# Two-stack transformer on one core: how TensorE is carried from one sublayer to the next

## What is computed

```python
x = x + rmsnorm(m, g[1])                       # m: attention (layer 0) or short convolution (layer 1)
f = sq_relu_mlp(rmsnorm(x, g[2]), w_mlp_up[i], w_mlp_down[i])
x = x + rmsnorm(f, g[3])
gate = sigmoid(rmsnorm(x, g[4]) @ w_ple_gate[i])
e = (p[i] @ w_ple_proj[i]) * gate
x = x + rmsnorm(e, g[5])
```

## Time and profile before

| | |
|---|---|
| median of 3 runs | 1717.42 us |
| lowest, highest | 1690.49, 1718.61 us |
| span of the profiled execution | 1691.7 us |
| TensorE matmuls busy | 1567.7 us (93%) |
| VectorE, ScalarE, GpSimd busy | 979.4, 724.6, 136.1 us |
| mean granted TensorE clock | 0.938 of full |

### The profile page before, as it was taken

How to read it: one execution, slowest core, us unless ns; L and a number is a source line. 1 busy time by engine, 2 the same in 40 slices (tenths; PEclk the granted TensorE clock), 3 DMA queues, 4 the chain that set the end, 5 groups by cost and what they waited for, 6 DMA issues and landing times.

```text
span 1691.7 us, 24256 instructions
## 1 busy us (share of the span) xinstructions
PE 1567.7 (93%) x9802; PEld 1373.8 (81%) x9802; DVE 979.4 (58%) x1251; ACT 724.6 (43%) x931; POOL 136.1 (8%) x112
## 2 busy tenths in 40 slices
PE   7999999977998999868989999989999799899998
PEld 7966899866988999657668888879999686689997
DVE  4554565555566655549776565655655475456554
ACT  4443554445445544435632222244444363345443
POOL 2000111100000111000212212000000020000000
PEclk8999999988999999988988999989999896699999
DMA  7612465543654555524530000026565352045553
GB/s 252 187 61 76 144 213 186 191 145 123 189 162 156 198 187 187 163 100 124 170 112 26 1 2 1 1 86 208 169 210 174 127 189 64 13 162 189 186 163 124
DMA packets 81823, 229.15 MB, mean 135 GB/s; under 512 B 11729, under 2 KB 17553, under 8 KB 81713
## 3 DMA queue, kind: packets, MB, share of 16 engines
q1 hardware_dynamic: 81584, 227.54, 41.7%
q0 software_dynamic: 128, 0.07, 0.0%
HBM read 226.46 MB, written 1.05 MB: 134 GB/s over the span
## 4 chain that ended last, share of the span: by engine, by line
PE 87%; DVE 8%; ACT 3%; issue 1%; POOL 1%; DMA 1%; SPq 0%; DVEq 0%; ACTq 0%; POOLq 0%
PE PS L404 50%; PE PS L407 33%; PE PS L419 4%; ACT SH L376 1%; DVE X L619 1%; DVE SL L382 1%; DVE LG L1341 1%; DVE XL L518 1%; ACT JK L597 0%; DVE XN L596 0%; DVE XI L1061 0%; POOL SM L609 0%; DVE SL L379 0%; DVE XT L1349 0%; DVE XT L1350 0%
## 5 line engine op out<-in xcount | busy, mean ns | idle before, releaser
L382 DVE SCALAR_TENSOR_TENSOR SL<-ST,SM,SH 128x1024 fp32r<-128x1024 f32 (+1 forms) x256 | 317.0, 1258 | 242.3 <-ACT SH L376 233.9
L404 PE MATMUL PS<-XH,SH 128*128 128x256 f32 x1568 | 443.7, 283 | 8.3 <-DVE XL L518 8.3
L407 PE MATMUL PS<-XH,SL 128*128 128x256 f32 x1568 | 444.5, 283 | 0.0
L404 PE MATMUL PS<-XL,SH 128*128 128x256 f32 x1568 | 443.3, 283 | 0.0
L376 ACT ACTIVATE SH<-ST,SM 128x1024 fp32r<-128x1024 f32 (+1 forms) x256 | 281.1, 1121 | 289.4 <-PE PS L407 271.8
L379 DVE TENSOR_TENSOR SL<-ST,SH 128x1024 fp32r<-128x1024 f32 (+1 forms) x167 | 213.5, 1295 | 171.4 <-ACT SH L376 154.1
L404 PEld LDWEIGHTS PS<-XH,SH 128*128 128x128 f32 x1568 | 301.3, 192 | 10.6 <-ACT XH L517 5.7
L404 PEld LDWEIGHTS PS<-XL,SH 128*128 128x128 f32 x1568 | 298.0, 190 | 0.6
L407 PEld LDWEIGHTS PS<-XH,SL 128*128 128x128 f32 x1568 | 298.1, 190 | 0.0
L376 ACT ACTIVATE SH<-ST 128x1024 fp32r<-128x1024 f32 (+1 forms) x167 | 172.1, 1047 | 193.4 <-PE PS L407 184.4
L404 PE MATMUL PS<-SH,XH 128*128 128x512 f32 (+1 forms) x432 | 178.1, 412 | 29.9 <-ACT XH L517 8.4
(11 more groups left out here) (306 smaller groups left out, 1744.3 us busy)
## 6 DMA issues: line engine op xcount, KB each, us to landing
ST<-in_ffn_w_gu SPq DMA_DIRECT2D x80, 512.0 KB, 4.7
ST<-in_w_mlp_up SPq DMA_DIRECT2D x64, 512.0 KB, 4.7
ST<-in_w_mlp_down SPq DMA_DIRECT2D x64, 512.0 KB, 4.3
ST<-in_ffn_w_down SPq DMA_DIRECT2D x44, 512.0 KB, 4.4
ST<-in_w_attn_in SPq DMA_DIRECT2D x24, 512.0 KB, 3.7
ST<-in_w_conv_in SPq DMA_DIRECT2D x24, 512.0 KB, 3.6
ST<-in_w_ple_gate SPq DMA_DIRECT2D x16, 512.0 KB, 3.6
ST<-in_kv_w SPq DMA_DIRECT2D x16, 512.0 KB, 4.4
```

Source lines behind the costliest of these rows:

```text
L382: b = ve.do(lambda e: e.scalar_tensor_tensor(l[p0:p1, 0:cols], t[p0:p1, 0:cols], sc, h[p0:p1, 0:cols].bitcast(F32), ALU.mult, ALU.subtract ...
L404: pe.go(lambda e: e.matmul(o, l, r, start=start, stop=stop, skip_group_check=skip))
L407: return pe.do(lambda e: e.matmul(o, l, r, start=start, stop=stop, skip_group_check=skip))
```

## The change

- The slots of split weights go from 5 to 6, stages from 5 to 4, parameter rows from 3 to 2, and up to 5 units are split ahead. Head and tail groups of `kind_a` are four units (`EDGE`); a tail has as many as the call gives, and beyond it nothing is split ahead. In a head group the splits are written one by one (`lazy`).
- The functions behind a sublayer are called for one m at a time (`chain(m)`). Two new functions call them: `enter_b` and `enter_a`. Both write, for every engine: chain of m = 0, fill, transposes and split of m = 0, chain of m = 1, and only then, after the first unit has been used on m = 0, the transposes and the split of m = 1.
- `enter_b` (five places) runs its first two units through `kind_b_halves`: each block is multiplied with 128 tokens at a time, so a unit takes 48 matmuls with 128 moving columns where it took 24 with 256.
- `keep_busy` multiplies constants into a free PSUM bank: two or four plain fp32 matmuls of 512 columns in each place, and ten of 128 columns at the start of the kernel.
- In the gates, the embedding's two units stand between the transposes of m = 0 and the chain of m = 1. The sigmoid, its product and the squares are cut into 512-column pieces.
- Lambda and its six DMAs are moved to the beginning of the kernel, behind the forget gate.

```diff
-NSPLIT, NSTAGE, NPAR = 5, 5, 3
+NSPLIT, NSTAGE, NPAR = 6, 4, 2
+EDGE = 4
 LOOK = NSPLIT - 1
...
-    def take_group(n):
+    def take_group(n, look=LOOK):
...
-        while n_split[0] <= min(i + LOOK, len(units) - 1):
+        while n_split[0] <= min(i + max(look, n - 1), len(units) - 1):
             unit_split()
         assert n_split[0] >= i + n
...
-    def kind_a(xs, kbs, banks, first=True, last=True, xt=None, end=False):
+    def kind_a(xs, kbs, banks, first=True, last=True, xt=None, end=False, mid=None, look=LOOK):
...
-        groups = [[k] for k in kbs]
-        if xt is not None and len(kbs) >= 3:
-            groups = [kbs[0:3]] + [[k] for k in kbs[3:]]
-        if end:
-            cut = sum(len(g) for g in groups) - 3
-            groups = [g for g in groups if g[-1] < kbs[0] + cut] + [kbs[cut:]]
+        head = EDGE if xt is not None and len(kbs) >= EDGE else 0
+        tail = min(EDGE, int(end) if end is not True else EDGE)
+        groups = ([kbs[0:head]] if head else []) + [[k] for k in kbs[head:len(kbs) - tail]] + ([kbs[len(kbs) - tail:]] if tail else [])
         assert sum(len(g) for g in groups) == len(kbs)
         for g in groups:
-            us = take_group(len(g))
+            lazy = xt is not None and g is groups[0]
+            us = [] if lazy else take_group(len(g), len(g) - 1 if end and g is groups[-1] else look)
             for m in range(2):
-                if xt is not None and g is groups[0]:
+                if lazy:
                     pe.wait(xt[m])
-                for k, (i, h, l) in zip(g, us):
+                for j, k in enumerate(g):
+                    if lazy and m == 0:
+                        us += take_group(1, 0)
+                    i, h, l = us[j]
                     pe.wait(split_tok[i])
                     for n in range(2):
                         ls = [x[:, k, m * 128:(m + 1) * 128] for x in xs]
                         rs = [x[:, n * 512:(n + 1) * 512] for x in (h, l)]
+                        if first and k == kbs[0]:
+                            pe.wait(bfree[banks[2 * m + n]])
                         tok[m] = mm3(bank(banks[2 * m + n]), ls, rs, first and k == kbs[0], last and k == kbs[-1])
+                    if lazy and mid is not None and m == 0 and j == 0:
+                        mid()
             for i, _, _ in us:
                 pe_done[i] = tok[1]
         return tok
...
+    def kind_b_halves(xs, banks, xt, mid, nblk=8, n=2):
+
+        us = take_group(n, n - 1)
+        for m in range(2):
+            pe.wait(xt[m])
+            for k, (i, h, l) in enumerate(us):
+                pe.wait(split_tok[i])
+                for f in range(nblk):
+                    c = (f % 2) * 256 + m * 128
+                    if m == 0 and k == 0 and f % 2 == 0:
+                        pe.wait(bfree[banks[f // 2]])
+                    ls = [x[:, f * 128:(f + 1) * 128] for x in (h, l)]
+                    rs = [x[:, k, m * 128:m * 128 + 128] for x in xs]
+                    tok = mm3(bank(banks[f // 2], c, c + 128), ls, rs, m == 0 and k == 0 and f % 2 == 0, False)
+                if m == 0 and k == 0:
+                    mid()
+                if m:
+                    pe_done[i] = tok
+
+    def ahead(n=1):
+
+        for _ in range(n):
+            if n_split[0] < len(units) and (n_split[0] < NSPLIT or n_split[0] - NSPLIT in pe_done):
+                unit_split()
+
+    def keep_busy(n, b, c=C_LV, w=512):
+
+        pe.wait(bfree[b])
+        for _ in range(n):
+            mm(bank(b, 0, w), CC[:, 0:128], CC[:, c:c + w], True, True)
+
...
+    keep_busy(10, 7, 0, 128)
...
+    def enter_b(chain, banks, fill):
+
+        r = [None, None]
+        chain(0)
+        keep_busy(*fill[0])
+        r[0] = raw_half(0, 0)
+        chain(1)
+        keep_busy(*fill[1])
+
+        def second():
+            r[1] = raw_half(1, 0)
+
+        kind_b_halves(XS[0], banks, r, second)
+        ahead(1)
+        return raw_rstd()
+
+    def enter_a(chain, base, banks, fill, between=None, **kw):
+
+        r = [None, None]
+        chain(0)
+        keep_busy(*fill)
+        r[0] = raw_half(0, base)
+        if between is not None:
+            between()
+        chain(1)
+        ahead(2)
+
+        def second():
+            r[1] = raw_half(1, base)
+
+        return kind_a(XS[0], range(8), banks, xt=r, mid=second, **kw)
...
+    ve.wait(tl)
+    for j in range(2):
...
+    def mlp(layer, chain, fill, tail_free):
+        rt = enter_b(chain, (4, 5, 6, 7), fill)
...
+            else:
+                t = kind_b(XS[0], range(2, 8), bs, first=False)
...
+        return down(3), pw, (PH, PL), [lb, lc]
...
+        def embed():
+            wait_banks([0, 1, 2, 3])
+            pe.wait(xs_tok)
+            emb.append(kind_a(xs, range(2), (0, 1, 2, 3), look=0))
+
+        tg = enter_a(mlp_chain, 4, (4, 5, 6, 7), (1, 0), embed, end=True)
...
+    rt = enter_b(ple_chain, (4, 5, 6, 7), ((2, 1), (2, 4)))
...
+    kind_b(XS[0], range(2, 4), (4, 5, 6, 7), first=False, last=False)
...
+    before = mlp(1, conv_chain, ((2, 4), (2, 4)), te0[1])
+    ple_chain, _ = ple(1, before)
+    for m in range(2):
+        ple_chain(m)
...
+    def ffn(chain):
+        rt = enter_b(chain, (4, 5, 6, 7), ((1, 2), (2, 3)))
...
+    t = enter_a(chain0, 0, (4, 5, 6, 7), (2, 2))
+    rt = raw_rstd()
```

More of the change, by code:

```diff
@@ L395, in take_group, with take @@
         return [(j, SH[j % NSPLIT], SL[j % NSPLIT]) for j in range(i, i + n)]
-    def take():
-        r = take_group(1)[0]
+    def take(look=LOOK):
+        r = take_group(1, look)[0]
         pe.wait(split_tok[r[0]])
@@ L459, in kind_b @@
         return tok
+    def kind_b_halves(xs, banks, xt, mid, nblk=8, n=2):
[23 more added lines that the diff above has]
+            mm(bank(b, 0, w), CC[:, 0:128], CC[:, c:c + w], True, True)
+    bfree = {b: None for b in range(8)}
     t_x = [dma_once(X[:, m, :], A["x"][0][m * 128:m * 128 + 128, :]) for m in range(2)]
@@ L933, in mlp @@
             bs = (0, 1, 2, 3) if g else (4, 5, 6, 7)
-            wait_banks(bs)
-            t = kind_b(XS[0], range(8), bs)
+            if g:
+                wait_banks(bs)
+                t = kind_b(XS[0], range(8), bs)
+            else:
+                t = kind_b(XS[0], range(2, 8), bs, first=False)
             if g == 3:
@@ L951, in ple @@
         te = emb.pop()
-        xt, rt = raw_t(4)
-        wait_banks([4, 5, 6, 7])
-        tg = kind_a(XS[0], range(8), (4, 5, 6, 7), xt=xt, end=True)
+        rt = raw_rstd()
         xfree[0] = tg[1]
-        ts = []
-        for m in range(2):
-            a = ac.do(lambda e, m=m: e.activation(SG[:, m, :], PS[:, 2048 + m * 1024:2048 + m * 1024 + 1024], ACT.Sigmoid, scale=small(500 + m)), tg[m], hr_free[0], rt)
-            b = ve.do(lambda e, m=m: e.tensor_tensor(EE[:, m, :], PS[:, m * 1024:m * 1024 + 1024], SG[:, m, :], ALU.mult), a)
-            bfree[4 + 2 * m] = bfree[5 + 2 * m] = a
-            bfree[2 * m] = bfree[2 * m + 1] = b
-            ts.append(b)
@@ L972, in emit @@
+        return chain, te
+    before = mlp(0, attn_chain, ((2, 3), (2, 3)), last_pe)
+    ple_chain, te0 = ple(0, before)
     t_cw = dma_once(small(208, 24), A["conv_wT"], d)
-    xt, rt = raw_t(0)
+    rt = enter_b(ple_chain, (4, 5, 6, 7), ((2, 1), (2, 4)))
     pw = powers(rt)
@@ L983, in emit @@
     hs = [slice(0, 4), slice(4, 8)]
-    pe.wait(xt)
-    wait_banks([4, 5, 6, 7])
-    kind_b(XS[0], range(3), (4, 5, 6, 7), last=False)
+    kind_b(XS[0], range(2, 4), (4, 5, 6, 7), first=False, last=False)
     tsb = row_scale(rt, 0)
     tsb = ve.do(lambda e: e.tensor_tensor(SBT[:, :], SBT[:, :], SBT[:, :], ALU.mult), tsb)
-    t = kind_b(XS[0], range(3, 8), (4, 5, 6, 7), first=False)
+    t = kind_b(XS[0], range(4, 8), (4, 5, 6, 7), first=False)
     sb4 = SBT[:, :].unsqueeze(1).to_broadcast([128, 4, S])
@@ L1600, in down @@
             pe.wait(hx[g])
-            t = kind_a(HX[g % 2], range(FG[g] // 128), (4, 5, 6, 7), first=g == 0, last=g == len(FG) - 1)
+            t = kind_a(HX[g % 2], range(FG[g] // 128), (4, 5, 6, 7), first=g == 0, last=g == len(FG) - 1, end=FG[g] // 128 if g == len(FG) - 1 else 0)
             hx_free[g % 2] = t[1]
@@ L1606, in ffn @@
             bs = (0, 1, 2, 3) if g else (4, 5, 6, 7)
-            wait_banks(bs)
             if g == 0:
-                pe.wait(xt)
-                kind_b(XS[0], range(3), bs, nblk=2 * n // 128, last=False)
+                kind_b(XS[0], range(2, 4), bs, nblk=2 * n // 128, first=False, last=False)
                 tsb.append(row_scale(rt, 0))
-                t = kind_b(XS[0], range(3, 8), bs, nblk=2 * n // 128, first=False)
+                t = kind_b(XS[0], range(4, 8), bs, nblk=2 * n // 128, first=False)
             else:
+                wait_banks(bs)
                 t = kind_b(XS[0], range(8), bs, nblk=2 * n // 128)
@@ L1707, in weave @@
         return t
+    t = enter_a(chain0, 0, (4, 5, 6, 7), (2, 2))
+    rt = raw_rstd()
     ve.wait(rt)
     ac.wait(rt)
-    wait_banks([4, 5, 6, 7])
```

(1 more changed line is left out.)

213 lines of the change are left out of this document (112 added, 101 removed).

## The result

| | before | after |
|---|---|---|
| median | 1718.0 us (4 runs, 1690.5 to 1718.8) | 1761.7 us (4 runs, 1756.9 to 1763.9) |
| after / before | | 1.043, 95% interval 1.039 to 1.047 |
| span of the profiled execution | 1691.7 us | 1762.1 us |

A forecast was written before the change was run, and what follows sets the result against it. TensorE was taken to bound the kernel. Losses at the `enter_b` places, less gains at gates, keys and values and RWKV, summed to +5.9 us on the median 1717.4: 1723 us, range 1680 to 1765.

The forecast's parts named there:

- The price of a matmul, 0.11 us: In the halves at `enter_b`: a 128-column matmul costs its weight load, 0.11 us, bounds 0.11 and 0.119.
- The queue working, 17.4 us for `kind_b` after a norm: Attention to MLP 0: the second half's chain waits in the queues, both units end at 17.4 us, before 14.4.
- Gates, keys and values, RWKV's projections: Gains at these handovers: gate 0 -4.5 us, gate 1 with RWKV projections -6.6, keys and values -8.9.
- Four stages hidden: Weight stages cut from five to four: 4 us of slack hide the loads, so no cost.
- the late-weights rival: Four stages bring weights late, 1 us a unit over some 100 units: 1820 us; chance 0.04.
- The end, -0.7 forecast: At the kernel's end: the last addition wins 0.7 us.
- The clock in the entries: At the five `enter_b` places: low clock charged as one restart, 2.1 us, at gate 0 to convolution.
- one restart of 2.1 us: Gate 0 to convolution: after a wait, 48 matmuls take 7.8 us instead of 5.7 at low clock.
- Halves above 0.2 us: Sign of a wrong forecast: 128-column matmuls at the `kind_b` entries above 0.2 us each instead of 0.11.
- The rival that had the mechanism and nearly the size: Low clock in the halves: 0.21 us a matmul, 9.6 us in each of five places, 1771 us; chance 0.11.
- The clock of the attention stages: Rival: either attention stage's clock flips, up to 27 us won (1696) or as much lost (1750); chance 0.18.
- Putting the sum on the median: The sum of +5.9 us was added to before's median, 1717.4, not to the profiled span, 1691.7.

The follow-up runs named there:

- halves_256: The kernel after, each matmul of the halves moving 256 columns (its 128 tokens twice, output not the reference's): 1700.6 and 1736.1 us.
- no_fill: The kernel after without the constant matmuls at the eight entries, those at the kernel's start kept: 1757.5 and 1756.1 us.
- before_again: The kernel before, unchanged, profiled a second time: 1715.8 and 1725.6 us, profiled span 1713.8 us.
- best1: Before's entry order, slots, stages, parameter rows and groups of three, with after's gates, keys and values, early lambda, plus 256-column constants per attention head: 1678.1 us.

## Why the prediction was wrong

- **The price of a matmul, 0.11 us: right.** 0.113 at the full clock, and 0.215 at the low one, where the earlier trace rows had 0.21. The Trainium skill's 81 ns (TensorE: Matmul & The Clock Gate, Back-to-back issue gap) is not what this stream shows; the forecast's own row was nearer.
- **The queue working, 17.4 us for `kind_b` after a norm: right** to 0.1 us in after's one undisturbed window. At the full clock the convolution's interval came to +4.4 for 3.7, MLP 1 to +3.7 for 3.1 (halves_256); the two networks to +10.1 and +9.5 for 7.9. There the working was some 2 us short each.
- **Gates, keys and values, RWKV's projections: right** in sign and nearly in size, -22.4 for -20.0.
- **Four stages hidden: wrong, but small.** "4 us of slack hide it" was worked out for the steady stream; in the burst behind feed-forward 0's entry ACT waited 2.2 and 1.7 us, and the interval cost 4.2 us more than with five stages (54.8 against 50.6, with slots and groups changed too). This is the late-weights rival in one place, not once a unit.
- **The end, -0.7 forecast: nothing came.** 4.9 us from the last down projection to the end in both.
- **The clock in the entries: the step that failed.** The sum held one restart of 2.1 us, at the convolution, and none at the other four; the low clock cost some 30 (after less halves_256). "Halves above 0.2 us" was a sign of being wrong that the forecast itself had named. The rival that had the mechanism and nearly the size (0.21 us each, 9.6 us a place, 1771) was given 0.11, "Against: it began with a gap, and the halves start behind full-length fills". Both reasons fell. The constants changed the sum of the entries by 4 us (no_fill). And the halves also start with a gap: at feed-forward 0, after's timeline has, behind the constants,

```profile
1176.37 1.27 DVE L1679 TENSOR_TENSOR X<-X,PS 128x512 f32<-128x512 f32 x2
1177.56 2.47 DVE L383 SCALAR_TENSOR_TENSOR SL<-ST,SM,SH 128x1024 fp32r<-128x1024 f32 x2
...
1178.98 0.43 PE L405 MATMUL PS<-XH,SH 128*128 128x128 f32 x1 [2.33 <-DVE SL L383]
```

  the first unit's split behind two additions, 2.33 us idle, and then the low clock for 27.3 us. The forecast had worked out this very wait (there `XL` is done at 3.6 and the first unit ready at 6.1; at the convolution 4.4 to 10.7) and had in the earlier trace rows a stream bound by weight loads that ran at 0.50 for nine busy microseconds. Together they should have given the rival more than 0.11. With its 9.6 us at four places the sum would have been 1762, but that this is the measured time is in part luck: three places stayed low for long (9.8, 7.6 and 10.6 us over halves_256), and 12 us lie outside the entries and the moved parts.
- **The clock of the attention stages** flips as the rival said, by 29 us for the 27 allowed, but in before too and whatever the change. One profile of each group of before's times shows it. Putting the sum on the median served the comparison, since after's profile has that stage at the low level too.

Against the forecast's own sum, on before_again's span: 48.3 us measured, 5.9 forecast. The entries are 59.4 above it for 25.6 forecast, 33.8 too much, most of it the clock (30 us, for the one restart of 2.1 that the sum held); the moved parts -23.0 for -20.0; the rest, 11.9 us, is differential attention and its output (7.5), RWKV (2.9) and the start (1.5, for 1.0 forecast). In differential attention kernels without constants there came to between 66 and 73 us, so those 7.5 us are not shown to be the change's.

## What to carry to other kernels

Before a matmul is cut into narrower ones to start it earlier, price it at both clock levels: here the cut, where the clock stayed up (halves_256), came out even with whole units in the same queue order (329.4 and 330.7 us over five entries) and 28 us behind whole units in the old order, and at 1.2 GHz it cost up to 10.6 us a place more, because the stream of 128-column matmuls in 19 of 30 entries did not get its clock back while it lasted. What pays at a boundary is work on the waiting engines' queues (both norm chains first, the next units' splits ahead of them, enough stages for the burst of splits behind the entry), not filling TensorE with constants. And where a kernel's times fall into two groups, compare two profiles stage by stage first: here one such comparison found an attention stage that takes 29 us more at the low clock, and best1, 40 us under before, has both the constants that kept that stage's clock up and the parts of the rebuilt boundaries that won.

## What the runs showed of the hardware

- A busy TensorE is not a fast one. With 100% of its time busy it ran at 1.2 GHz for 27.3 us, most of it matmuls of 128 columns, and the level rose 5.2 us after the first one of 256 (1201.1 to 1206.3). With 256 columns in the same places, halves_256 was low at one entry only, for 6.8 us, and rose among the halves there.
- The same instructions keep either level. The first attention stage took 62.6 us wholly at 1.00, or 91.7 with 68.3 of them at 0.50, in executions of one kernel. It was low in eleven of thirteen profiles without constants in it; with 16 constant matmuls of 256 columns it was at 1.00, or nearly, in each of the three profiles that had them (0.98, 1.00, 1.00), and so it was in the two with half as many columns.
- At the full level 16, 128 and 256 columns cost 0.110, 0.113 and 0.119 us a matmul, so these streams are bound by something other than the columns, most likely the weight load that each matmul has. At the low level a half costs 0.215 us, 1.9 times as much, near the ratio of the clocks.
